# Gate table of a PEER layer: three of a slice's eight tokens weighed by GpSimd instead of VectorE

## The reference, cut to what matters

```python
def peer(xn, w_q, sub_keys, u, v):
    q = (xt @ w_q).reshape(t, PEER_HEADS, 2, PEER_HALF)
    sc = jnp.einsum("thpc,hpnc->thpn", q, sub_keys).astype(jnp.float32)
    top_s, top_i = lax.top_k(sc, PEER_TOPK)
    ...
    best_s, best_pos = lax.top_k(cand_s, PEER_TOPK)
    idx = jnp.take_along_axis(cand_i, best_pos, axis=-1)
    gate = jax.nn.softmax(best_s, axis=-1)
    ...
        act = jnp.einsum("cd,ced->ce", xc, uc).astype(jnp.float32)
        hid = (jax.nn.gelu(act, approximate=False) * gc).astype(xc.dtype)
        return jnp.einsum("ce,ced->cd", hid, v[ic])
```

## Time and profile before

| | us |
|---|---|
| median of 3 runs | 2348.16 (2347.37 to 2349.66) |
| profiled execution | 2344.72 |
| its span, first to last instruction | 2342.9 |
| PE busy in the span | 2201.5 (94%) |
| DVE busy | 1530.2 (65%) |
| ACT busy | 864.4 (37%) |
| POOL busy | 436.2 (19%) |

### The profile page before, as it was taken

How to read it: one execution, slowest core, us unless ns; L and a number is a source line. 1 busy time by engine, 2 the same in 40 slices (tenths; PEclk the granted TensorE clock), 3 DMA queues, 4 the chain that set the end, 5 groups by cost and what they waited for, 6 DMA issues and landing times. The chain is left out here.

```text
span 2342.9 us, 29399 instructions
## 1 busy us (share of the span) xinstructions
PE 2201.5 (94%) x11221; PEld 1907.0 (81%) x11221; DVE 1530.2 (65%) x2699; ACT 864.4 (37%) x1431; POOL 436.2 (19%) x308
## 2 busy tenths in 40 slices
PE   7999899898999889888999999999998999989898
PEld 6777788687999889878788888999996798877667
DVE  4545433425999979864888888688887624435644
ACT  3345323222333644863333333333334332222322
POOL 0100000000122010001434335266661000012200
PEclk9999999899999999999999999999998999989999
DMA  5221233202778574678999999799993322210220
GB/s 220 100 86 55 70 119 144 78 13 88 233 252 254 172 240 148 194 227 280 357 385 384 385 384 367 253 360 362 354 331 117 126 89 91 90 54 1 108 99 36
DMA packets 211836, 451.32 MB, mean 193 GB/s; under 512 B 13808, under 2 KB 133616, under 8 KB 204912
## 3 DMA queue, kind: packets, MB, share of 16 engines
q1 hardware_dynamic: 174832, 315.21, 39.2%
q0 software_dynamic: 36864, 134.23, 15.8%
HBM read 404.56 MB, written 44.83 MB: 192 GB/s over the span
## 5 line engine op out<-in xcount | busy, mean ns | idle before, releaser
L1598 PE MATMUL bank<-Vh,Hh 128*128 128x512 f32 x768 | 300.3, 391 | 4.3 <-DVE Hl L1681 4.1
L1600 PE MATMUL bank<-Vh,Hl 128*128 128x512 f32 x768 | 300.5, 391 | 0.0
L1599 PE MATMUL bank<-Vl,Hh 128*128 128x512 f32 x768 | 300.4, 391 | 0.0
L929 PE MATMUL bank<-XH,Ue 128*128 128x384 f32 x672 | 233.9, 348 | 26.4 <-DVE Ue L918 26.4
L1620 ACT ACTIVATE Vh<-Vr 128x1024 fp32r<-128x1024 f32 x128 | 135.9, 1061 | 303.1 <-PE bank L1600 288.5
L967 POOL DMA_INDIRECT ring<-in_v,gidx x128 | 205.4, 1605 | 165.0 <-DVE x_res L979 68.8
L930 PE MATMUL bank<-XL,Ue 128*128 128x384 f32 x672 | 228.3, 340 | 0.0
L931 PE MATMUL bank<-XH,Ue 128*128 128x384 f32 x672 | 228.0, 339 | 0.0
L1676 DVE TENSOR_TENSOR Vl<-Vr,Vh 128x1024 fp32r<-128x1024 f32 x128 | 156.4, 1222 | 51.2 <-ACT Vh L1620 49.2
L967 POOL DMA_INDIRECT ring<-in_u_rows,gidx x92 | 114.9, 1248 | 385.3 <-DVE ghid L972 203.8
L1598 PEld LDWEIGHTS bank<-Vh,Hh 128*128 128x128 f32 x768 | 144.7, 188 | 34.9 <-DVE Hl L1681 6.0
(11 more groups left out here) (380 smaller groups left out, 4963.2 us busy)
## 6 DMA issues: line engine op xcount, KB each, us to landing
Vr<-in_v SPq DMA_DIRECT2D x128, 512.0 KB
ur<-in_u SPq DMA_DIRECT2D x86, 512.0 KB
W<-in_w_stream SPq DMA_DIRECT2D x19, 2048.0 KB, 8.3
Gr<-gates SPq DMA_DIRECT2D x32, 768.0 KB
XT<-in_u SPq DMA_DIRECT2D x42, 512.0 KB
early<-ar SPq DMA_DIRECT2D x84, 192.0 KB
A<-early SPq DMA_DIRECT2D x84, 192.0 KB
xs<-in_w_mixer SPq DMA_DIRECT2D x14, 1024.0 KB
```

The lines of the kernel that those rows point to most:

```text
L929: pe.matmul(ps, h[:, k], c.Xh[:, k, 0:DN], start=k == 0, stop=False)
L1598: pe.matmul(ps, Hh[r][:, tok], Vh[r][:, cut], start=p == 0, stop=False)
L1599: pe.matmul(ps, Hh[r][:, tok], Vl[r][:, cut], start=False, stop=False)
L1600: mm = pe.matmul(ps, Hl[r][:, tok], Vh[r][:, cut], start=False, stop=p == PK - 1)
```

## The change

VectorE's multiplication of tokens 5 to 7 and its wait for `hot_made` are taken out of the slice loop. GpSimd gets a function `weigh(tt)` for the 16 slices of a tile: for each it waits until both comparisons of the slice are done, multiplies each of the three tokens by its gate with one `tensor_scalar` of 128 x 128 elements (the gate is a column of `ijg`, one value a partition), and signals `weighed_d` behind the third. GpSimd's 36 fetches are split: the first 28, then the slices of tile 0, then 8 fetches, then the slices of tiles 1 and 2.

```diff
@@ -1195,8 +1195,23 @@
             pool.memset(ones, 1).then_inc(onesd, 1)
             pool.wait_ge(gat.ready, 1)
-            for s in range(DOTS_TABLE):
+
+            def weigh(tt):
+                for j in range(tt * NSL, (tt + 1) * NSL):
+                    pool.wait_ge(hot_made, 2 * j + 2)
+                    for k in range(ON_ACT, S):
+                        one = hot[0][j % 2][:, k]
+                        last = pool.tensor_scalar(one, one, ijg[:, 2, j * S + k:j * S + k + 1], None, ALU.mult)
+                    last.then_inc(weighed_d, 1)
+
+            first = DOTS[0] + DOTS[1] + DOTS[2] + RG - 1
+            for s in range(first):
                 gat.fetch(pool, s)
+            weigh(0)
+            for s in range(first, DOTS_TABLE):
+                gat.fetch(pool, s)
+            weigh(1)
+            weigh(2)
@@ -1459,9 +1474,6 @@
                     for half in (1, 0):
                         dve.tensor_tensor(hot[half][r], mid(c.iota, S), bc(ijg[:, half, tok:tok + S], P), ALU.is_equal).then_inc(hot_made, 1)
-                    dve.wait_ge(hot_made, 2 * j + 2)
-                    some = hot[0][r][:, ON_ACT:]
-                    dve.tensor_tensor(some, some, bc(ijg[:, 2, tok + ON_ACT:tok + S], P), ALU.mult).then_inc(weighed_d, 1)
                     fill(0, e + 1 + (j - tt * NSL + 3) * E_SLICES // NSL)
```

## The result

The changed kernel takes 2405.46 us (median of 4 runs, 2400.94 to 2408.27) against 2348.91 us before, a ratio of 1.0247 with a 95% interval of 1.0231 to 1.0263. That is 56.6 us slower. The direction was forecast. The size, 21.6 us, was not: the time lies above the range of 2347 to 2396 us.

A forecast was written before the change was run, and what follows sets the result against it. A ring of waits through VectorE, ScalarE and TensorE, 13.53 us per four slices, was taken as the bound; 12 rounds x 1.8 us (1.5 + 0.3) = 21.6 us on 2348.16 gave 2369.8 us, range 2347 to 2396.

The forecast's parts named there:

- VectorE's relief: Slice stages: removing 48 VectorE multiplications frees 22.6 us of work, all beside ScalarE's weighing, so booked at 0 us.
- The rival in which VectorE was the bound: Slice stages: VectorE's relief counts, so faster, 2325.6 us, or 2335 us if ScalarE and TensorE stop it; chance 0.07.
- The product's price: GpSimd's 128 x 128 multiplication, three a slice: 0.30 us each, the middle of 0.20 and 0.39.
- near bounds: Limits for GpSimd's product: below, memset 0.204 us and 4-column tensor_scalar 0.192; above, two-input instruction scaled to 128 columns, about 0.39.
- The far row: Profile row of a GpSimd tensor_scalar of 40 columns that ran once, 0.608 us; treated as out of line.
- The turns on the ports: Slices: GpSimd's products and VectorE's two-input instructions alternate on shared SBUF ports; +1.5 us weighing, +0.3 us VectorE delay a round.
- The case that I had put aside: Seen in the scan at 2167.94: three VectorE instructions passed undisturbed while GpSimd's instruction took 5.31 us against 1.90.
- The chain from comparison to products: Slices, where two comparisons follow: 1.06 + 0.30 + 1.13 + 0.60, 3.1 us, against 1.63 for ScalarE's weighing with handover.
- The clock: TensorE in the slices: longer waits can bring stretches at its lower level, 1.2 GHz; named under a slower rival, not priced.
- the ring: Waits among VectorE, ScalarE and TensorE that close in 13.53 us per four slices, without VectorE's multiplication of three tokens.
- GpSimd becomes the bound: Rival, slices: 0.6 us products or three VectorE instructions passing; about 36 us slower, up to twice that, 2384 to 2420; chance 0.12.
- GpSimd's queue: Fetch 28 stands behind tile 0's 48 products, with some 25 us of cover against 1 us; booked at 0.

The follow-up runs named there:

- experiment 2: Kernel before without VectorE's multiplication and TensorE's wait for it, nothing given to GpSimd (gates of three of eight tokens left out): 2347.23 us, ratio 1.0.
- experiment 1: Changed kernel with comparisons reading the row of numbers from PSUM: 2351.63 us, ratio 1.002; same edit on the kernel before as control: 2346.52 us, 0.9998.
- experiment 3: Changed kernel with six more TensorE products of 128 x 384 a slice, into an unread bank, ahead of its wait for GpSimd: 2390.93 us, ratio 1.0183.
- experiment 4: Changed kernel with GpSimd's three products of a slice put into one tensor_tensor of 128 x 384: 2350.26 us, ratio 1.0021.
- experiment 5: Changed kernel with one token on GpSimd and two on VectorE (one multiplication of 128 x 256): 2350.52 us, ratio 1.0019.

## Why the prediction was right in direction and wrong in size

**VectorE's relief is worth 0 us:** right, shown by experiment 2 with rounds of 13.53 us. The rival in which VectorE was the bound is out.

**The product's price:** wrong. I took 0.30 us between 0.20 and 0.39; it is 0.60, twice that and above both near bounds. I had taken the middle between a memset and a tensor_tensor scaled down by its columns, 0.39 us. The instruction with two inputs does come out near that scale (3 x 128 columns take 0.83 us, 4 x 128 take 1.04, so by their slope some 0.4 at 128, an estimate), but the `tensor_scalar` with one gate a partition doesn't lie below it. The far row has nearly the same time, 0.608 us; its instruction has two constants and 40 columns, and the same form took 0.192 at 4, so the agreement may be chance. With 0.60 for 0.30 the three products take 1.8 us and end behind ScalarE's 1.57 even when the ports are free, and the second and third come late enough to meet VectorE's next pair.

**The turns on the ports:** wrong in one half. I let GpSimd in between the two comparisons of a pair, with 0.3 us of delay to VectorE. It got in there in three places only; 19 products waited for two VectorE instructions (1.94 us in the pair of slices above), and VectorE's comparisons took 1.36 us at most (ns min/median/max below):

```profile
L1476 DVE TENSOR_TENSOR W<-tab_sb,ijg x96: 1210/1221/1361, 775.9 to 1086.8; 128x1024 f32<-128x1024 f32 x96
```

The case that I had put aside, several instructions of VectorE that pass in a row, was the nearer one; here it was two, not three. The chain from comparison to products was 3.8 us (788.88 to 792.68), not 3.1.

**The clock:** this is the term that I put at nothing. I named it among the causes of a still slower kernel, at no price; TensorE's products then took 18.9 us more, a third of the 59.2. In the pair of slices above, 9.95 us = 2.46 (comparisons) + 3.80 (weighing) + 3.69 (TensorE). Against the ring's 2.39 + 1.63 + 2.08, weighing costs 2.17 us more and the slower clock 1.61. I had booked 1.5 + 0.3 in all.

**How often:** I counted once in a round of four slices, so 12 times, and 1.8 us each; a round took 4.9 us more. TensorE's waits put down to "issue" are 20. 20 x 2.17 = 43 us of longer weighing is close to the 40.3 us that TensorE idled more, against 21.6 in the forecast. 20 x 1.61 = 32 us would be too much for the clock: the products cost 18.9 us more, because the lower clock meets only a part of the late slices for all of their time. The two parts aren't independent causes, though: without the ports' conflict only some 5 us remain in all (experiment 1), and with a steadier clock 43 (experiment 3), because the pause of TensorE that brings the clock down is itself the work of the ports.

**The range:** my case "GpSimd becomes the bound" had the right product price and the wait for several of VectorE's instructions, and gave 2384 to 2420 us; the result lies in the middle of it. I gave it 0.12 and cut it in half with the range. The row of 0.608 us alone should have made it larger. That the result falls into this case's middle is in part luck: its sum, too, had nothing for the clock, and came to the height of the result only by counting up to twice a round.

**The rule of the Trainium skill** (SBUF — State Buffer, section "SBUF: two separate sides"), by which a VectorE instruction with two SBUF inputs and a GpSimd instruction that reads SBUF shut each other out, is borne out by experiments 1 and 4 as to which instructions get in each other's way. That the one that starts first shuts the other out for its whole instruction agrees with VectorE's instructions in the traces. With GpSimd's it doesn't: the product that ran from 788.88 to 789.48 overlapped the pair that began at 789.25 and took its undisturbed 2.36 us, and a product of 0.60 us lengthened a comparison by 0.14 us at most. The measurement decides.

**GpSimd's queue:** right. The first fetches behind the slices of tile 0 came at 852.33 and 854.57, and the selection for tile 2 took 87.76 us for 87.60.

**What stays open:** the profiled span grew by 3.8 us more than the table phase did. The part behind the table, which no edit touches, took 1286.5 us for 1281.9; no experiment isolates that, and it is within the spread of the runs (2400.94 to 2408.27). I haven't shown either by what rule GpSimd gets the ports between two VectorE instructions: it did so in some places of the scan, in three pairs of comparisons of the changed kernel, in nine of experiment 5, and in others not.

## What to carry to other kernels

An engine that is busiest in a stage isn't its bound if it waits in each round: add up the ring of waits from start to start, and look whether the instruction that you want to move is in it. Before work goes to GpSimd, see which VectorE instructions stand beside it with two inputs in SBUF, and whether one of these can come from PSUM; here that edit alone turned a loss of 57 us into one of 5. Give GpSimd one instruction with many columns instead of several short ones (experiment 4, 2350.3 us for 2405.5), and price a TensorE pause with the slower products that follow it, not only with its length.

## What the runs showed of the hardware that I had not expected

- GpSimd's `tensor_scalar` with one gate a partition takes 0.60 us at 128 columns, so three take 1.76 us. One `tensor_tensor` over 384 columns does the same in 0.83 us, and over 512 columns it takes 1.04 us.
- Two instructions of VectorE without a wait between them mostly let no GpSimd product in that started while the first was running: it lasted up to 2.74 us in place of 0.60. In three pairs of the changed kernel it got in between, with 1.64 to 1.67 us. With one input from PSUM the same comparisons take as long as before (1.22 us) and don't stop it.
- The reverse is cheap for VectorE with short products (0.14 us at most) and dearer with long ones: `lo` took 1.74 us for 1.22 behind a multiplication of 384 columns.
- After a pause of 2.42 us TensorE's next 16 passes ran at the lower level of its clock and took 3.66 us for 1.95. It doesn't follow every time: after the same pause, at 978.17 and 1080.78, they took 2.02 us. Six idle products a slice kept the granted clock at 0.97 in the slices of tile 0.
